# The last turned block and v's turn stand next to scores in each attention head

## The reference

```python
q, k, v, z = jnp.split(h @ w_in, 4, axis=-1)            # 16 heads, q and k in two halves of 64, v 128
q = rms_norm(q.reshape(b, s, DA_HEADS, 2, DA_HEAD), q_norm_g) * (DA_HEAD ** -0.5)
k = rms_norm(k.reshape(b, s, DA_HEADS, 2, DA_HEAD), k_norm_g)
for blk in range(s // Q_BLOCK):                          # 4 blocks of 128 queries, causal
    scores = jnp.einsum('bqhmd,bkhmd->bhmqk', qb, kb)    # m: the two halves
    probs = jax.nn.softmax(scores + bias[None, :, None], axis=-1)
    weights = probs[:, :, 0] - lam * probs[:, :, 1]
    outs.append(jnp.einsum('bhqk,bkhe->bqhe', weights.astype(v.dtype), vb))
o = rms_norm(o, head_norm_g) * (1.0 - lam_0)
o = o.reshape(b, s, BRANCH) * jax.nn.silu(z)
return x + o @ w_out
```

## Time and profile before

| | |
|---|---|
| runs | 1898.75, 1902.66, 1902.66 us, median 1902.66 |
| the profiled execution | 1900.43 us, span 1898.6 |
| PE busy | 1869.9 us, 98% |
| DVE busy | 995.5 us, 52% |
| ACT busy | 818.2 us, 43% |
| POOL busy | 124.0 us, 7% |
| granted TensorE clock | 0.997 of full speed |
| attention rounds 0 to 18 | up to about 510 us of the span |

### The profile page before, as it was taken

One profiled execution on the slowest core, in us unless ns is written; L12 is line 12 of the kernel. 1 busy time (PEld: TensorE's weight loads), 2 busy tenths in 40 slices (PEclk: granted clock), 3 DMA queues, 4 the chain that ended last, 5 costly groups with the idle time before them and its releaser, 6 DMA issues.

```text
span 1898.6 us, 22387 instructions
## 1 busy us (share of the span) xinstructions
PE 1869.9 (98%) x8923; PEld 1448.7 (76%) x8923; DVE 995.5 (52%) x1778; ACT 818.2 (43%) x1328; POOL 124.0 (7%) x148
## 2 busy tenths in 40 slices
PE   8999999999999999999999999999999999999997
PEld 6566666666788788888886777778888878888886
DVE  6667666665544653333346667845434763333322
ACT  6566656656643342222324655434432442222221
POOL 0101111110001000000010011000000100000000
PEclk9999999999999999999999999999999999999999
DMA  5534333332233132222323313221123323222221
GB/s 199 182 127 162 137 144 145 146 143 101 78 132 114 67 111 100 95 95 93 100 87 124 104 65 106 70 92 35 45 89 111 124 90 103 94 100 97 92 93 62
DMA packets 56526, 201.95 MB, mean 106 GB/s; under 512 B 6478, under 2 KB 6934, under 8 KB 55784
## 3 DMA queue, kind: packets, MB, share of 16 engines
q1 hardware_dynamic: 44616, 158.32, 23.7%
q0 software_dynamic: 11808, 42.21, 6.1%
HBM read 195.23 MB, written 5.28 MB: 106 GB/s over the span
## 4 chain that ended last, share of the span: by engine, by line
PE 84%; DVE 8%; ACT 6%; issue 2%; DMA 0%; SPq 0%; DVEq 0%; ACTq 0%
PE ps L1202 24%; PE ps L1205 23%; PE ps L1203 23%; ACT wH L1908 2%; PE ps L1302 2%; PE ps L1338 1%; DVE a L1620 1%; DVE wL L1497 1%; PE ps L1266 1%; ACT a L2007 1%; PE ps L1290 1%; PE ps L1278 1%; PE ps L1345 1%; DVE g1a L1497 1%; PE ps L1255 1%
## 5 line engine op out<-in xcount | busy, mean ns | idle before, releaser
L1202 PE MATMUL ps<-hH,wH 128*128 128x512 f32 (+1 forms) x1560 | 635.7, 408 | 1.0 <-DVE hL L1568 1.0
L1205 PE MATMUL ps<-hH,wL 128*128 128x512 f32 (+1 forms) x1560 | 610.3, 391 | 1.0 <-DVE wL L1497 0.7
L1203 PE MATMUL ps<-hL,wH 128*128 128x512 f32 (+1 forms) x1560 | 608.7, 390 | 0.0
L1497 DVE TENSOR_TENSOR wL<-wr,wH 128x1024 fp32r<-128x1024 f32 (+2 forms) x285 | 343.9, 1207 | 490.8 <-ACT wH L1908 490.2
L1908 ACT ACTIVATE wH<-wr 128x1024 fp32r<-128x1024 f32 (+2 forms) x285 | 295.2, 1036 | 234.3 <-PE ps L1205 220.4
L1202 PEld LDWEIGHTS ps<-hH,wH 128*128 128x128 f32 (+1 forms) x1560 | 292.5, 187 | 97.0 <-issue 36.2
L1205 PEld LDWEIGHTS ps<-hH,wL 128*128 128x128 f32 (+1 forms) x1560 | 292.3, 187 | 67.5 <-DVE wL L1497 3.9
L1203 PEld LDWEIGHTS ps<-hL,wH 128*128 128x128 f32 (+1 forms) x1560 | 292.9, 188 | 60.7 <-issue 6.5
L1202 PE MATMUL ps<-gffn,wH 128*128 128x512 f32 x400 | 156.9, 392 | 1.0 <-DVE xT L1675 0.8
L1205 PE MATMUL ps<-gffn,wL 128*128 128x512 f32 x400 | 155.7, 389 | 0.0
L1203 PE MATMUL ps<-gffn,wH 128*128 128x512 f32 x400 | 155.6, 389 | 0.0
(11 more groups left out here) (304 smaller groups left out, 2079.4 us busy)
## 6 DMA issues: line engine op xcount, KB each, us to landing
wr<-wst SPq DMA_DIRECT2D x268, 512.0 KB, 3.4
a<-wfd POOLq DMA_DIRECT2D x54, 512.0 KB, 4.8
xT<-wfd POOLq DMA_DIRECT2D x18, 512.0 KB, 6.8
wr<-wst SPq DMA_DIRECT2D x16, 384.0 KB, 2.9
xT<-xin SPq DMA_DIRECT2D x8, 256.0 KB, 7.5
xT<-xin SPq DMA_DIRECT2D x2, 1024.0 KB, 6.3
xsave<-xT SPq DMA_DIRECT2D x1, 2048.0 KB, 7.3
c<-wfd POOLq DMA_DIRECT2D x8, 256.0 KB, 3.4
```

Source lines behind the costliest of these rows:

```text
L1202: e.matmul(o, hi, xh[k], start=k == 0, stop=False)
L1203: e.matmul(o, hi, xl[k], start=False, stop=False)
L1205: i = e.matmul(o, lo, xh[k], start=False, stop=k == t.nk - 1)
L1497: e.tensor_tensor(dst, x, hi.bitcast(F32), ALU.subtract).then_inc(s[name], 1)
```

## The change

Two entries of the table SCHED change: v's turn goes from step 10 to step 14, where the scores of block 2 are, and turnw of key block 3 from step 13 to step 9, where the scores of blocks 0 and 1 are. Within a step the order is by kind: the v turn comes before the scores, and turnw after them (and before an adaLN unit).

```diff
-SCHED = {"rstd": 1, "v": 10, "table": 2, "c": [(9, (0, 1)), (14, (2,)), (18, (3,))], "w": [11, 12, 16, 21],
-         "c0": [(14, (0, 1)), (17, (2,)), (20, (3,))], "w0": [16, 17, 19, 22], "d": [4, 7, 7, 13], "pv": 18, "ada": 30,
+SCHED = {"rstd": 1, "v": 14, "table": 2, "c": [(9, (0, 1)), (14, (2,)), (18, (3,))], "w": [11, 12, 16, 21],
+         "c0": [(14, (0, 1)), (17, (2,)), (20, (3,))], "w0": [16, 17, 19, 22], "d": [4, 7, 7, 9], "pv": 18, "ada": 30,
          "o": 5, "lo": (12, 18)}
```

## The result

| | before | changed |
|---|---|---|
| median of 12 runs | 1902.66 us | 1905.68 us |
| lowest and highest | 1898.75, 1903.84 | 1903.80, 1906.68 |
| ratio, 95% interval | | 1.0018 (1.0011 to 1.0026) |
| profiled execution | 1900.43, span 1898.6 | 1905.86, span 1904.1 |
| PE, DVE, ACT busy | 1869.9, 995.5, 818.2 | 1869.4, 997.0, 818.3 |

The change makes the kernel 0.18% slower, 3.4 us by the ratio and 3.0 by the medians. In a second measurement it was 1.0024 (1.0015 to 1.0034), which is 4.6 us by the ratio and 3.5 by the medians. The busy time of all engines is the same within 1.5 us: nothing more is done, it only ends later.

The account below looks back on a forecast made before the run. PE and the DVE and ACT chain were both taken to bound the attention rounds. Of 8.1 us gross stall, 2.1 (ordinary rounds) + 2.2 (adaLN rounds) = 4.3 us remained, giving 1907.0 us from the median, range 1900.8 to 1911.0.

Parts of the forecast that it names:

- 1. The places: Turns on PE beside scores instead of between products: no cheaper or dearer, 0.0 us, bounds 6 us either way.
- 2. The stall: PE at step 9 waits for ACT to empty block 1's turn bank: 0.54 us a round, 15 rounds, 8.1 gross.
- 3. DVE: DVE from block 1's scores to block 2's, its two copies in swapped order: sum stays 3.67 us, cost 0.
- 4. The absorption: PE's waits in the next rounds shrink and take up part of the stall, leaving 2.1 + 2.2 = 4.3 us.
- six ordinary rounds: Those before rounds 3, 5, 6, 10, 12, 13: next waits absorb 0.19 each, leaving 2.1 us in all.
- Rounds 3 and 10: ACT copies a mod row in the next rounds, 4 and 11; waits of 0.52 to 0.57 there leave 0.0.
- Rounds 8 and 15: In next rounds 9 and 16 PE waits for DVE's copy of o at step 1; 0.78 leaves 0.
- Rounds 7 and 14: An adaLN unit stands between scores groups and DVE waits for PE: stall counts in full, 0.54 each.
- B: Rival: the chain alone sets ordinary rounds' pitch, so only the four adaLN rounds pay; +2.2 us, chance 0.15.
- C: Rival: nothing absorbs the stall, the chain being delayed with PE in all rounds; +8.1 us, chance 0.12.
- E: Rival: the bank at step 9 is free in time, so no wait arises; 0.0 us, chance 0.09.
- D: Rival: turns between products have a hidden 0.20 us price that the new places save; -1.7 us, chance 0.06.

Follow-up runs that it names:

- last10_v14: The change with the last turned block at step 10 instead of 9, v's turn still at 14; 1902.44 us, ratio 0.9999 to the kernel before.
- behind: Kernel before with v's turn and the last block's turn both behind the scores of block 2 at step 14; 1892.31 us, ratio 0.9949.
- late_bank: The change with the two turns' banks swapped, so the last block takes that of block 2's turn; 1909.47 us, ratio 1.0035 to the kernel before.
- v14: Kernel before with only v's turn moved, to step 14, the last block staying at 13; 1902.85 us, ratio 1.0003.
- last9: Kernel before with only the last turned block moved, to step 9, v's turn staying at 10; 1905.65 us, ratio 1.0019.
- after_ada16: The change with the adaLN units of rounds 6, 7, 13, 14 moved to step 16; 1901.04 us, ratio 0.9998 to the kernel before.
- ada16: Kernel before with the adaLN units of rounds 6, 7, 13, 14 moved to step 16; 1897.87 us, ratio 0.9979.
- behind_ada16: Kernel before with both turns behind block 2's scores and the four adaLN units at step 16; 1889.56 us, ratio 0.9935.

## Why the prediction was right, and where it was off

The direction, the mechanism and the order of size held: forecast +4.3 us, measured +3.0 and +3.5 by the medians, inside the range. By its steps:

**1. The places.** 0.0 was right for v's turn: last10_v14 has it in front of the scores and costs 0.05 us over fifteen rounds. The place behind scores is not free of effect: five transpositions there cost 0.08 less in `behind`. For the single one of the change the stall hides it.

**2. The stall.** Forecast 0.54 a round from the end of ACT's copy; measured 0.56 in round 4 (0.68 less 0.12). The bank read from the ring was the right one: moving the turn one step (last10_v14) and giving it the other bank (late_bank) moved the cost as the end of ACT's copies does.

**3. DVE.** The sum of 3.67 us stayed to the hundredth, and the hole, filled in the change, showed where the small copy was missing (v14).

**4. The absorption.** The six ordinary rounds were put at 0.35 each and came to 0.28 to 0.42, 2.2 in all for 2.1. Rounds 3 and 10: 0.0 and 0.02 forecast, 0.00 and 0.07 measured. Rounds 8 and 15: 0 and 0. Rounds 6 and 13: 0.54, measured 0.57 and 0.59. Two terms were too small. Rounds 7 and 14 were put at 0.54 and cost 0.76 and 0.75, since I had named the adaLN unit as queued behind the stall but not priced the turn between two groups of another form. And round 16 cost 0.20 where I had 0; but 0.14 of that comes back at the turns of step 7 in round 17, behind the end of the table, so that only 0.06 was missing. Less these 0.14, the stall costs 4.95 us over all rounds, not 4.3.

**What the forecast had not: the clock.** A stretch of 3.4 us at 1.2 GHz near 1290 us, in the delta rule nearly 800 us behind the last moved instruction, is in all three profiles of the kernel before and in neither of the change. Its absence gives 1.5 us back. So the nearness of 4.3 to the measured 3.4 owes something to luck, to two errors of opposite sign: the stall put 0.65 too low, and 1.5 of the clock not foreseen.

The rivals. B (+2.2) and C (+8.1) both fall by the table, which has the 0.3 to 0.4 of ordinary rounds that neither gives. E (no wait) falls by last9 and by the row with its wait of 0.55. D (the places save 0.20 a group) falls by last10_v14 for v's turn and by last9 for the last block: alone, it costs all of the 5.1.

## What to carry to other kernels

When steps are moved in a list that hands out buffers in order, work out first which buffer each step now gets and when its last reader is done: here a turn moved four steps forward met a bank that was emptied 0.56 us too late, and one step later it cost nothing. A stall on the busiest engine costs what is left after its next waits, round by round, so measure those waits before summing. And to find out what a small move does, compare the lengths of like rounds in the traces (good to some 0.03 us) and not only run times, which here hid 2.1 us in one kernel and added 3.5 in another.

## What the runs showed of the hardware

The clock near 1290 us is the one surprise. PE stands still for 1.5 us there, waiting for DVE, in the kernel before and in the changed one alike. These are the rows that end this wait, in the kernel before (again) and in the changed one:

```profile
1289.26 0.22 PE L1402 MATMUL ps<-a 32*32 32x32 f32 x2 [1.50 <-DVE a L1836]
1294.56 0.22 PE L1402 MATMUL ps<-a 32*32 32x32 f32 x2 [1.50 <-DVE a L1836]
```

Beginning 1 to 2 us after its end, TensorE was granted 1.2 GHz for 3.4 us in all three profiles of the kernel before, in last10_v14 and in after_ada16, and not in the changed kernel, last9, v14, late_bank, behind, ada16 or behind_ada16, though the instructions of that part are the same. The kernels differ there only in when they come to it, and the two groups don't mix: the five with the stretch end this wait 1287.6 to 1289.3 us from the start, the eight without it at 1283.4 or before, or at 1291.8 or later. Why the time should decide is open; a kernel's time can move by 1.5 us through it without any work having changed.

The other drop goes with a longer wait. It is near 58 us, in eight of the thirteen profiles, and PE has waited 2.0 to 2.8 us for DVE in round 1 there. Here is the kernel before again, where the scores behind that wait take 2.08 us instead of 1.13:

```profile
58.15 2.08 PE L1266 MATMUL ps<-a 64*128 64x512 f32 x4 [2.32 <-DVE tiny L1620]
```

The wait alone does not decide. The first profile of the kernel before has the same one, of 2.32 us and ending at 58.08, and its scores take 1.13; ada16 (2.35) and after_ada16 (2.08) have no stretch either. In behind and behind_ada16 the wait is 1.4 and 1.3, without a stretch. The Trainium skill ("TensorE: Matmul & The Clock Gate", What's actually happening) says that the window in which activity is judged is free-running and that the moment of a change therefore varies from run to run. The two profiles of the kernel before at 58 us agree with it; the clean division of the thirteen near 1290 us is not what it would lead one to expect.
